# Queries of the recurrence, and keys and queries of stick-breaking attention, as seven products of quarters

## The chip, the core and the metric

One core of a Trainium2 chip runs the whole program once. The metric is device microseconds per execution. Engines: TensorE (PE; its weight loads are PEld), VectorE (DVE), ScalarE (ACT), GpSimd (POOL), and SyncE (SP), which issues the large DMA transfers. Each engine executes its own instructions in program order; engines wait for one another by semaphores.

## What is computed

Two layers of a hybrid mixer with an MLP (256 rows, width 1024, float32), then a block with three attentions and a mixture of experts. The change is in the mixer's projections of each of the two layers:

```python
h = rms_norm(x, norm_mix[l])
(sq, sk, sv, dq, dk, dv, iq, ik, iw, hq, hf, hi, hg,
 g_sb, g_dsa, g_hg) = jnp.split(h @ w_in_l, ...)
z = einsum('bqhd,bkhd->bhqk', sq, sk) * scale   # stick-breaking scores, 6 heads of 64
score = sum over 8 heads of iw * relu(iq @ ik)  # then the top 64 keys of each row
q = silu(hq); f = lb + (1 - lb) * sigmoid(hf)   # the recurrence, 4 heads of 128
```

`hq` and `hf` have 512 columns, `sk` and `sq` 384 each, and the three gates `g_*` 3072 together.

## The kernel before

The weights of `w_in` come in chunks of up to 512 columns into a ring of four slots; SyncE issues a chunk when the last reader of the chunk four before it is done (`last_use`, `used`). The order of chunks is `hf`, `hq`, `sk`, `sq`, then six gate chunks.

**Two ways to make a projection.** `feature_major` (line 1141) makes a tile of 128 features for 256 rows: eight matmuls over the depth of 1024, each 128x128 against 256 moving columns, into one PSUM bank. Each float32 matmul stands as two instructions in the trace. The other way, used for `hf` and the last eight gate tiles, is `gate_product` (line 1302): the weight is cut in four quarters (features by depth), the rows of h in four, and seven products of sums of quarters (`m1` to `m7`, in `GATE_ORDER`) replace eight. A *unit* `(c, t2)` has seven products of four matmuls with 128 moving columns, in two banks, `gy` (m1, m5, m4) and `gx` (m2, m6, m7, m3), and gives 256 features. VectorE makes the four sums of weight quarters (`gate_weight_sums`, lines 2466 to 2471) and the sums of row quarters; after a unit ScalarE copies m1 to SBUF (step `gc`), VectorE adds the products up in four instructions (`gate_corner_sums`, lines 2492 to 2498), which frees both banks, and ScalarE's step `gf` takes the corners on.

**The order.** `mixer_steps` writes one list, `MIX`, by hand, and TensorE, ScalarE and VectorE each walk it, doing what a step asks of that engine. Before the change its head is: the two units of `hf` with their corners; query tile `hq` 0; nine turns `rt` and the reversal `hj`; `hq` 1 to 3; `hp` (VectorE: forget gate); half of the first eight indexer products `ix` (128 rows against 128 keys); `sk` 0; the other half; `tk` 0 (VectorE: top 64 of the first block); `sk` 1, 2 and `sq` 0 to 2; `t5` (in layer 0 alone: a bias table, VectorE lines 2599 and 2601); eight `ix` of the second block; `tk` 1; `z`, three pairs of score products (lines 1390 and 1392); then gate columns `g` and the rest.

**What paces `ix`.** Each product goes to a bank; ScalarE puts its relu into one of two buffers (line 2016), waiting for VectorE's use of the buffer two before; VectorE multiplies by the head's weight and adds (lines 2638, 2640). The top-k is lines 2650 to 2657.

**Banks.** `Banks.give` hands out six PSUM banks in turn (`RING`); a step's first matmul waits until the user six gives before has freed its bank. Two further banks are given with `long=True`, in turn, to results that stand for longer.

**Evictions.** ScalarE takes a sigmoid of each `hq` tile (line 1982) and VectorE multiplies the tile by it (line 2595); ScalarE copies `sk` and `sq` tiles to `skT` and `sqT` (lines 1984, 1986). `z` waits for these copies.

Of the kernel before, what the change touches and what calls it, by code (L numbers as in the profile page):

```python
# [84 lines left out]
FM = {n: (n, w - 1) for n, _, w in PROJ[-4:]}  # L85
# [100 lines left out]
SEVENS = ("hf", 4, 5)  # L186
# [3 lines left out]
def mixer_steps():  # L190
# [87 lines left out]
def build(nc, a, out):  # L278
    ctx = ExitStack()
    with ctx:  # L280
# [182 lines left out]
        gate_rows_sums = [Cutter(region, REGION, at).cut(4, 4, P) for at in (at_os, at_R)]  # L463
        gate_corners = [Cutter(region, REGION, at_f + 1024 + 1024 * j).cut(8, P) for j in range(2)]

        gT_flat = gT.rearrange("p m t -> p (m t)")
        t5_onehot, t5_tab = gT_flat[0:32, 2048:3584], gT_flat[0:32, 5120:5132]
# [5 lines left out]
        def oT2(c):  # L473
# [3 lines left out]
            if c < 6:  # L477
# [58 lines left out]
         quarter_sums_ready, row_sums_ready, seven_m1_copied, seven_sigmoids) = [sem(n) for n in (  # L536
# [9 lines left out]
             "quarter_sums_ready row_sums_ready seven_m1_copied seven_sigmoids").split()]  # L546
# [35 lines left out]
        def seven_chunk(c):  # L582

            return c if c in FM else ("g", c)

        for l in range(DEPTH):
# [251 lines left out]
        def gate_weights(l, c):  # L838

            w = slot(chunk_at[(l, seven_chunk(c))])  # L840
            return [[w[:, 4 * kh:4 * kh + 4, 256 * fh:256 * fh + 256] for kh in range(2)] for fh in range(2)]

        def gate_sums(l, c):

            own_, a21 = own_quarters, gate_weights(l, c)[1][0]
            if c in ("hf", 4):
                return own_[:, 0], own_[:, 1], a21, own_[:, 2]
# [2226 lines left out]
```

## Time and profile before

| | |
|---|---|
| median of 3 runs | 1594.91 us (1593.36 to 1595.44) |
| profiled execution, span from first to last instruction | 1592.4 us (its total time is not given) |
| busy share of the span | TensorE 92%, VectorE 47%, ScalarE 20% |
| mean granted TensorE clock | 0.962 of full |

A timeline's rows merge equal instructions in a row: start, length of the stretch, engine, line, operation, output and inputs, how many, and in brackets the idle time before and what ended it. Layer 0 of the mixer lies at about 80 to 250 us, layer 1 at 550 to 720.

### The profile page before, as it was taken

The page shows a single profiled execution, that of the slowest core. Times are in us where ns is not written, and L with a number is a line of the kernel's source. Part 1 is how long each engine was busy: PE and PEld are TensorE (multiplying, and loading weights), DVE is VectorE, ACT ScalarE, POOL GpSimd, SP SyncE. Part 2 cuts the span into 40 slices and gives each one's busy share as a digit, 9 for nine tenths or more (in the row PEclk, how much of TensorE's full clock was granted, in tenths as well). Part 3 has the DMA queues.
Part 4 walks back from the last instruction along what each step waited for, and adds up shares of the span by engine and source line. Part 5 has one row for each costly group of instructions (what it writes and reads, how often), then busy time and mean ns, then how long its engine had stood idle before and what let it go on. Part 6 is the DMA issues. An engine that isn't in the chain of part 4 may idle for free.

```text
span 1592.4 us, 19689 instructions
## 1 busy us (share of the span) xinstructions
PE 1458.7 (92%) x8156; PEld 1004.4 (63%) x8156; DVE 740.9 (47%) x1465; ACT 314.6 (20%) x655; POOL 22.7 (1%) x41
## 2 busy tenths in 40 slices
PE   8999999999999999999999999999999576577578
PEld 5687889999545788898999446755554133133132
DVE  3646576766666646567666656544331000001001
ACT  2234431122001125430222001334410000000000
POOL 0000000000000000000000002100000000000000
PEclk9999999999999999999999999999999788788689
DMA  9547224454453633334444446655799999999998
GB/s 319 191 159 245 90 100 153 157 199 169 158 175 108 213 127 138 107 107 159 159 169 182 179 158 204 226 185 186 287 392 426 427 426 426 428 427 426 428 419 318
DMA packets 114921, 380.17 MB, mean 239 GB/s; under 512 B 10836, under 2 KB 23252, under 8 KB 104144
## 3 DMA queue, kind: packets, MB, share of 16 engines
q1 hardware_dynamic: 111952, 369.53, 60.6%
q0 software_dynamic: 2880, 9.36, 1.9%
q8 instruction: 67, 1.10, 0.3%
q14 instruction: 22, 0.18, 0.0%
HBM read 377.25 MB, written 5.73 MB: 241 GB/s over the span
## 4 chain that ended last, share of the span: by engine, by line
PE 79%; DMA 17%; DVE 2%; SPq 1%; ACT 1%; issue 1%; DVEq 0%; ACTq 0%
DMA ring<-in_w 17%; PE bank L1508 13%; PE bank L1561 12%; PE bank L1144 11%; PE bank L1151 8%; PE bank L1324 5%; PE bank L1712 4%; PE bank L1298 3%; PE bank L1250 3%; PE bank L1274 2%; PE bank L1610 2%; PE bank L1738 1%; PE bank L1481 1%; PE bank L1483 1%; PE bank L1200 1%; PE bank L1226 1%
## 5 line engine op out<-in xcount | busy, mean ns | idle before, releaser
L1144 PE MATMUL bank<-hT,ring 128*128 128x256 f32 x832 | 185.4, 381 | 0.0
L1144 PEld LDWEIGHTS bank<-hT,ring 128*128 128x128 f32 x832 | 156.0, 190 | 21.9 <-issue 1.0
L1712 PE MATMUL bank<-ring,region 128*32 128x512 f32 x208 | 116.4, 724 | 48.8 <-DMA region<-in_w 48.8
L1712 PE MATMUL bank<-region 128*32 128x512 f32 x512 | 116.6, 722 | 48.5 <-DMA ring<-in_w 48.5
L1561 PE MATMUL bank<-region 128*128 128x512 f32 x320 | 140.6, 592 | 0.0
L1561 PEld LDWEIGHTS bank<-region 128*128 128x128 f32 x320 | 60.5, 190 | 74.6 <-issue 74.6
L1508 PE MATMUL bank<-region 128*128 128x128 f32 x768 | 100.5, 275 | 0.0
L1508 PEld LDWEIGHTS bank<-region 128*128 128x128 f32 x768 | 93.0, 192 | 0.0
L1712 PEld LDWEIGHTS bank<-region 128*32 128x32 f32 x512 | 29.1, 130 | 94.0 <-issue 94.0
L1712 PEld LDWEIGHTS bank<-ring,region 128*32 128x32 f32 x208 | 25.8, 130 | 83.3 <-issue 83.3
L1151 PE MATMUL bank<-ring,hT 128*128 128x512 f32 x160 | 71.7, 596 | 0.0
L1771 PE MATMUL bank<-region 128*32 128x512 f32 x192 | 56.3, 684 | 15.9 <-DMA hT<-in_w 14.1
L2944 DVE TENSOR_TENSOR region<-bank,region 128x512 f32<-128x512 f32 x8 | 5.5, 692 | 139.1 <-ACT region L2113 139.1
L1508 PE MATMUL bank<-hT,ring 128*128 128x128 f32 x512 | 67.3, 275 | 0.0
L1712 PE MATMUL bank<-own_slot,region 128*32 128x512 f32 x112 | 63.4, 730 | 0.0
L1508 PEld LDWEIGHTS bank<-hT,ring 128*128 128x128 f32 x512 | 62.3, 192 | 0.1
L2954 DVE TENSOR_TENSOR region<-bank,region 128x512 f32<-128x512 f32 x8 | 5.5, 692 | 113.0 <-PE bank L1712 93.1
L1668 PEld LDWEIGHTS bank<-region,x 128*128 128x128 f32 x224 | 54.1, 335 | 5.9 <-issue 5.9
L1561 PE MATMUL bank<-ring,region 128*128 128x512 f32 x128 | 57.5, 592 | 0.0
L1151 PE MATMUL bank<-ring,region 128*128 128x456 f32 (+1 forms) x128 | 55.6, 591 | 1.4 <-ACT region L1853 1.4
L1668 PE MATMUL bank<-region,x 128*128 128x128 f32 x224 | 55.4, 405 | 0.0
L1771 PE MATMUL bank<-ring,region 128*32 128x512 f32 x256 | 54.9, 637 | 0.0
(488 smaller groups left out, 2421.6 us busy)
## 6 DMA issues: line engine op xcount, KB each, us to landing
region<-in_w SPq DMA_DIRECT2D x43, 2048.0 KB, 38.6
ring<-in_w SPq DMA_DIRECT2D x30, 2048.0 KB, 37.7
ring<-in_w_in SPq DMA_DIRECT2D x26, 2048.0 KB, 8.2
ring<-in_w_up SPq DMA_DIRECT2D x16, 2048.0 KB, 8.3
ring<-in_w_down SPq DMA_DIRECT2D x32, 1024.0 KB, 6.3
own_slot<-in_w SPq DMA_DIRECT2D x7, 2048.0 KB, 43.3
ring<-in_w_out SPq DMA_DIRECT2D x6, 2048.0 KB, 7.9
region<-in_w SPq DMA_DIRECT2D x22, 512.0 KB, 9.3
```

The lines of the kernel that those rows point to most:

```text
L1144: t = mm(b[:, 0:T], w[:, k, :], act[:, k, :], start=(k == 0), stop=(k == KD - 1))
L1151: t = mm(b[:, 0:cols], act(k)[:, i * P:(i + 1) * P], w[:, k, :], start=(k == 0), stop=(k == KD - 1))
L1250: t = mm(b, left[:, k, :], right[:, k, :], start=(k == 0), stop=(k == 3))
L1274: t = mm(b, left[:, k, :], right[:, k, :], start=(k == 0), stop=(k == 3))
L1298: t = mm(b, left[:, k, :], right[:, k, :], start=(k == 0), stop=(k == 3))
L1324: t = mm(b, left[:, k, P * t2:P * t2 + P], right[:, k, :], start=(k == 0), stop=(k == 3))
L1508: t = mm(b, left[:, k, P * t2:P * t2 + P], right[:, k, :], start=(k == 0), stop=(k == 3))
L1561: t = mm(b[:, :], left[:, t2, :], right[:, t2, :], start=(c4 == 0 and t2 == 0), stop=(c4 == 7 and t2 == 1))
L1610: t = mm(b[:, :], oT2(k)[:, i * P:(i + 1) * P], slot(chunk_at[(2, ("wo", n))])[:, k, :], start=(k == WO_FIRST), stop=(k == WO_LAST))
L1668: t = mm(b[:, P * k:P * k + P], x_rows[:, i, 4 * n + k, :], pick[:, i, :], start=(i == 0), stop=(i == NT - 1))
L1712: t = mm(b[32 * e:32 * e + 32, :], xg[:, k, 32 * e:32 * e + 32], four[e][c][:, 512 * (k % 2):512 * (k % 2) + 512], start=(k == 0), stop=(k ...
L1771: t = mm(outs[n][32 * e:32 * e + 32, :], aTq[:, c, 32 * e:32 * e + 32], w[e][:, 512 * n:512 * n + 512], start=(c == 0), stop=(c == 3))
```

## The change

The joined group `skq` treats the 384 columns of `sk` and the 384 of `sq` as the two feature halves of one weight: three units give keys and queries of two heads each. `hq` becomes two units. `hq`'s weight sums are made ahead of the list; `skq`'s in two parts (`gw`), the first between `hf`'s first and second corners, the second after the latter, since two of the sums overwrite those of `hf`. The turns and the reversal move ahead of all of `hq`. The second half of the first `ix` comes after the second `skq` unit, and the corners of the second and third `skq` units after `tk` 0. The second units of `hf` and `skq` use the two long banks. ScalarE's `gf` for `hq` is one sigmoid of 512 columns, and VectorE multiplies; for `skq` it is two copies of 256 columns out of the corners. `skq`'s corners lie in the place of the gates. The core of the diff (places of buffers, semaphores and the choice of quarters are left out):

```diff
@@ -183,7 +182,18 @@
 LAST = LEVELS - 1
-SEVENS = ("hf", 4, 5)
+SEVENS = ("hf", "hq", "skq", 4, 5)
+SEVEN_TILES = {"hf": 2, "hq": 2, "skq": 3, 4: 2, 5: 2}
+SIGMOIDS = ("hf", 4, 5)
+def seven_no(c, t2):
+    return sum(SEVEN_TILES[b] for b in SEVENS[:SEVENS.index(c)]) + t2
+SEVEN_UNITS = seven_no(SEVENS[-1], SEVEN_TILES[SEVENS[-1]])
@@ -198,14 +208,20 @@
         return [("gm", c, t2, m) for m in products]
+    def whole(c, t2):
+        return gm(c, t2, *GATE_ORDER)
+    def corners(c, t2):
+        return [("gc", c, t2), ("gf", c, t2)]
     s = []
-    s += gm("hf", 0, *GATE_ORDER) + [("gc", "hf", 0), ("gf", "hf", 0)]
-    s += gm("hf", 1, *GATE_ORDER) + [("gc", "hf", 1), ("gf", "hf", 1), ("hq", 0)]
-    s += [("rt", c) for c in range(9)] + [("hj",)] + [("hq", m) for m in range(1, 4)]
-    s.append(("hp",))
+    s += whole("hf", 0) + corners("hf", 0) + [("gw", "skq", 0)] + whole("hf", 1)
+    s += [("rt", c) for c in range(9)] + [("hj",)] + corners("hf", 1) + [("gw", "skq", 1)]
+    s += whole("hq", 0) + corners("hq", 0) + whole("hq", 1) + corners("hq", 1) + [("hp",)]
     half = N_IDX // 2
-    s += [("ix", 0, j) for j in range(half)] + [("sk", 0)] + [("ix", 0, j) for j in range(half, N_IDX)] + [("tk", 0)]
-    s += [("sk", m) for m in (1, 2)] + [("sq", m) for m in range(3)] + [("t5",)]
+    s += whole("skq", 0) + [("ix", 0, j) for j in range(half)] + corners("skq", 0)
+    s += whole("skq", 1) + [("ix", 0, j) for j in range(half, N_IDX)] + [("tk", 0)] + corners("skq", 1)
+    s += whole("skq", 2) + corners("skq", 2) + [("t5",)]
@@ -608,19 +633,18 @@
             for s in MIX:
-                if s[0] in ("rt", "hj", "ix", "hl", "hx", "ho", "oht", "o") or s[0] in FM:
+                if s[0] in ("rt", "hj", "ix", "hl", "hx", "ho", "oht", "o"):
                     bk.give((l,) + s)
-                    if s in FM.values():
-                        used((l, s[0]), (l,) + s)
...
                     if s[3] in GATE_STARTS:
-                        bk.give((l, GATE_STARTS[s[3]]) + s[1:3])
-                    if s[2:] == (1, GATE_ORDER[-1]):
-                        used((l, seven_chunk(s[1])), (l, "gy", s[1], 1))
+                        bk.give((l, GATE_STARTS[s[3]]) + s[1:3], long=s[1:3] in (("hf", 1), ("skq", 1)))
+                    if s[2:] == (SEVEN_TILES[s[1]] - 1, GATE_ORDER[-1]):
+                        for part in seven_chunks(s[1]):
+                            used((l, part), (l, "gy") + s[1:3])
@@ -1383,8 +1410,8 @@
                     elif kind == "z":
-                        c = s[1]
-                        wait_freed([(l, n, c) for n in ("sq", "sk")])
+                        c, rows = s[1], [slice(HD * hh, HD * hh + HD) for hh in range(2)]
+                        pe.wait_ge(heads_copied, 3 * l + c + 1)
@@ -1960,11 +1987,25 @@
                     elif kind == "gc":
-                        A_(gate_corners[s[2]][:, 6, :], read((l, "gy") + s[1:])[:, 0:P], ACT.Copy).then_inc(seven_m1_copied, 1)
+                        A_(seven_corners(*s[1:])[:, 6, :], read((l, "gy") + s[1:])[:, 0:P], ACT.Copy).then_inc(seven_m1_copied, 1)
+                    elif s[:2] == ("gf", "hq"):
+                        t2 = s[2]
+                        act.wait_ge(*bk.freed((l, "gy", "hq", t2)))
+                        if t2 == 0:
+                            act.wait_ge(row_corners_used, l + 1)
+                        else:
+                            act.wait_ge(hq_made, 2 * l + 1)
+                        A_(hsg_both, gate_corners[t2][:, 0:4, :].rearrange("p m t -> p (m t)"), ACT.Sigmoid).then_inc(sig_ready, 1)
+                    elif s[:2] == ("gf", "skq"):
+                        t2 = s[2]
+                        act.wait_ge(*bk.freed((l, "gy", "skq", t2)))
+                        halves = seven_corners("skq", t2)[:, 0:4, :].rearrange("p (f i) t -> p f (i t)", f=2)
+                        A_(skT[:, t2, :], halves[:, 0], ACT.Copy)
+                        A_(sqT[:, t2, :], halves[:, 1], ACT.Copy, scale=HD ** -0.5).then_inc(heads_copied, 1)
...
                         act.wait_ge(*bk.freed((l, "gy", c, t2)))
-                        dst = fT if c in FM else gT[:, 4 * c:4 * c + 4, :]
+                        dst = fT if c == "hf" else gT[:, 4 * c:4 * c + 4, :]
@@ -2457,18 +2487,27 @@
                 t.then_inc(wo_added, 1)
-            def gate_weight_sums(l, c):
-                dve.wait_ge(*arrive[chunk_at[(l, seven_chunk(c))]])
+            def gate_weight_sums(l, c, part=None):
+                for n in seven_chunks(c):
+                    dve.wait_ge(*arrive[chunk_at[(l, n)]])
...
                 s1, s2, s3, s4 = gate_sums(l, c)
-                n = 12 * l + 4 * SEVENS.index(c)
+                n = 4 * (len(SEVENS) * l + SEVENS.index(c))
+                if part == 1:
+                    dve.wait_ge(quarter_sums_ready, n + 2)
+                    V.tensor_tensor(s2, s1, a11, ALU.subtract).then_inc(quarter_sums_ready, 1)
+                    dve.wait_ge(quarter_sums_ready, n + 3)
+                    V.tensor_tensor(s4, a12, s2, ALU.subtract).then_inc(quarter_sums_ready, 1)
+                    return
...
                 dve.wait_ge(quarter_sums_ready, n + 1)
-                V.tensor_tensor(s2, s1, a11, ALU.subtract).then_inc(quarter_sums_ready, 1)
+                if part is None:
+                    V.tensor_tensor(s2, s1, a11, ALU.subtract).then_inc(quarter_sums_ready, 1)
                 V.tensor_tensor(s3, a11, a21, ALU.subtract).then_inc(quarter_sums_ready, 1)
-                dve.wait_ge(quarter_sums_ready, n + 2)
-                V.tensor_tensor(s4, a12, s2, ALU.subtract).then_inc(quarter_sums_ready, 1)
+                if part is None:
+                    dve.wait_ge(quarter_sums_ready, n + 2)
+                    V.tensor_tensor(s4, a12, s2, ALU.subtract).then_inc(quarter_sums_ready, 1)
@@ -2481,21 +2520,26 @@
             def gate_corner_sums(l, c, t2):
-                n = 6 * l + 2 * SEVENS.index(c) + t2
-                if n >= 2:
-                    dve.wait_ge(seven_sigmoids, n - 1)
+                if c == "hq":
+                    dve.wait_ge(seven_sigmoids, 6 * l + t2 + 1)
+                elif c == "skq":
+                    if t2 == 2:
+                        dve.wait_ge(heads_copied, 3 * l + 1)
+                elif (l, c) != (0, "hf"):
+                    dve.wait_ge(seven_sigmoids, 6 * l + 2 * SIGMOIDS.index(c) + t2 - 1)
+                four = seven_corners(c, t2)
                 x_, y_ = read((l, "gx", c, t2)), read((l, "gy", c, t2))
-                eight = gate_corners[t2].rearrange("p (a b) t -> p a b t", a=2)
-                pairs = gate_corners[t2].rearrange("p (a b) t -> p a b t", b=2)
+                eight = four.rearrange("p (a b) t -> p a b t", a=2)
+                pairs = four.rearrange("p (a b) t -> p a b t", b=2)
                 m5, m4 = y_[:, P:2 * P], y_[:, 2 * P:3 * P]
-                dve.wait_ge(seven_m1_copied, n + 1)
-                link(V.tensor_tensor(eight[:, :, 0, :], bc(gate_corners[t2][:, 6, :].unsqueeze(1), [2, P]),
+                dve.wait_ge(seven_m1_copied, SEVEN_UNITS * l + seven_no(c, t2) + 1)
+                link(V.tensor_tensor(eight[:, :, 0, :], bc(four[:, 6, :].unsqueeze(1), [2, P]),
                                      x_[:, 0:T].rearrange("p (a t) -> p a t", a=2), ALU.add))
-                free(V.tensor_tensor(eight[:, :, 1, :], bc(gate_corners[t2][:, 4, :].unsqueeze(1), [2, P]),
+                free(V.tensor_tensor(eight[:, :, 1, :], bc(four[:, 4, :].unsqueeze(1), [2, P]),
...
                 V.tensor_tensor(pairs[:, 0:2, 1, :], eight[:, :, 1, :], bc(m5.unsqueeze(1), [2, P]), ALU.add)
-                free(V.tensor_tensor(gate_corners[t2][:, 2, :], gate_corners[t2][:, 5, :], m4, ALU.subtract),
+                free(V.tensor_tensor(four[:, 2, :], four[:, 5, :], m4, ALU.subtract),
@@ -2578,10 +2622,11 @@
                 for i in range(NT):
-                    dve.wait_ge(sig_ready, 6 * l + i + 1)
+                    dve.wait_ge(sig_ready, 4 * l + i + 1)
...
                 t.then_inc(row_corners_used, 1)
+                gate_weight_sums(l, "hq")
@@ -2590,9 +2635,12 @@
                         free(V.tensor_copy(RT[:, s[1], :], read(key)[:, 0:T]), key)
-                    elif kind == "hq":
-                        dve.wait_ge(sig_ready, 6 * l + s[1] + 3)
-                        free(V.tensor_tensor(hqT[:, s[1], :], read(key)[:, 0:T], hsg[s[1] % 2], ALU.mult), key)
+                    elif s[:2] == ("gf", "hq"):
+                        t2 = s[2]
+                        dve.wait_ge(sig_ready, 4 * l + t2 + 3)
+                        V.tensor_tensor(hqT.rearrange("p (f t) n -> p t f n", f=2)[:, t2],
+                                        gate_corners[t2][:, 0:4, :].rearrange("p (f i) t -> p f (i t)", f=2),
+                                        hsg_both.rearrange("p (f n) -> p f n", f=2), ALU.mult).then_inc(hq_made, 1)
```

## Rows read from the trace of the kernel before

**Rows 1.** The page: busy time of the engines; granted clock in 40 slices.

```profile
PE 1458.7 (92%) x8156; PEld 1004.4 (63%) x8156; DVE 740.9 (47%) x1465; ACT 314.6 (20%) x655; POOL 22.7 (1%) x41
...
PEclk9999999999999999999999999999999788788689
```

**Rows 2.** Timeline of TensorE, layer 0: start us, us, engine, line, operation, xcount [idle before].

```profile
78.93 1.95 PE L1324 MATMUL bank<-hT,ring 128*128 128x128 f32 x16
...
91.44 3.62 PE L1144 MATMUL bank<-hT,ring 128*128 128x256 f32 x16
94.89 2.31 PE L1368 MATMUL bank<-region 128*128 128x128 f32 x18
...
97.47 10.52 PE L1144 MATMUL bank<-hT,ring 128*128 128x256 f32 x48
107.93 0.71 PE L1424 MATMUL bank<-region 64*128 64x128 f32 x8
...
131.32 2.73 PE L1381 MATMUL bank<-region 32*4 32x512 f32 x6
...
139.95 14.08 PE L1144 MATMUL bank<-hT,ring 128*128 128x256 f32 x64
```

**Rows 3.** The same for TensorE in layer 1.

```profile
550.62 1.95 PE L1324 MATMUL bank<-hT,ring 128*128 128x128 f32 x16
...
608.66 14.08 PE L1144 MATMUL bank<-hT,ring 128*128 128x256 f32 x64
```

**Rows 4.** Timeline of VectorE, layer 0.

```profile
81.63 0.17 DVE L2265 TENSOR_TENSOR small<-small 128x4 f32<-128x4 f32 x1 [7.92 <-ACT small L1953]
...
113.11 2.73 DVE L2640 SCALAR_TENSOR_TENSOR region<-region,small 128x128 f32<-128x128 f32 x7
115.87 0.23 DVE L2650 TENSOR_SCALAR region<-region 128x128 f32<-128x128 f32 x1
...
132.44 0.68 DVE L2599 TENSOR_TENSOR region<-bank,region 4x512 f32<-4x512 f32 x1 [9.41 <-PE bank L1381]
```

**Rows 5.** Timeline of VectorE, layer 1.

```profile
604.29 0.35 DVE L2638 TENSOR_SCALAR region<-region,small 128x256 f32<-128x256 f32 x1 [9.57 <-ACT region L2016]
```

**Rows 6.** Timeline of VectorE, layer 0: an add of weight quarters.

```profile
62.55 1.23 DVE L2466 TENSOR_TENSOR own_slot<-ring 128x1024 f32<-128x1024 f32 x1 [5.22 <-DMA ring<-in_w_in]
```

**Rows 7.** DMA issues within 66 to 79 and 78 to 90: count, KB, us to landing.

```profile
ring<-in_w_in SPq DMA_DIRECT2D x1, 2048.0 KB, 7.8
...
ring<-in_w_in SPq DMA_DIRECT2D x1, 1536.0 KB, 6.7
```

**Rows 8.** Timeline of all engines, layer 0: corner sums of `hf`.

```profile
85.38 0.28 ACT L1963 ACTIVATE region<-bank 128x128 f32<-128x128 f32 x1 [1.36 <-PE bank L1324]
...
85.79 0.42 DVE L2492 TENSOR_TENSOR region<-region,bank 128x256 f32<-128x256 f32 x1 [0.74 <-ACT region L1963]
...
87.04 0.28 DVE L2498 TENSOR_TENSOR region<-region,bank 128x128 f32<-128x128 f32 x1
87.36 0.63 ACT L1968 ACTIVATE region<-region 128x512 f32<-128x512 f32 x1 [0.40 <-DVE region L2498]
```

**Rows 9.** Timeline of ScalarE, layers 0 and 1.

```profile
95.43 1.14 ACT L1990 ACTIVATE region<-bank 128x256 f32<-128x256 f32 x3
...
603.80 0.66 ACT L2016 ACTIVATE region<-bank 128x256 f32<-128x256 f32 x2 [0.30 <-PE bank L1424]
```

**Rows 10.** Busy time by stretch: us, PE, PEld, DVE, ACT, POOL, PEclk, DMA, GB/s.

```profile
1224.00:1227.00 3.00, 0.91 (x10) 0.74 (x13) 1.09 (x3) 0.60 (x1) 0.00 (x0) 1.00 1.07 451
...
1243.00:1246.50 3.50, 0.00 (x1) 0.03 (x1) 0.00 (x0) 0.00 (x0) 0.00 (x0) 0.50 1.03 440
1246.50:1249.00 2.50, 2.50 (x12) 0.66 (x16) 0.00 (x0) 0.00 (x0) 0.00 (x0) 0.50 1.00 426
...
1266.00:1270.00 4.00, 3.91 (x20) 1.15 (x24) 0.00 (x0) 0.00 (x0) 0.00 (x0) 0.50 1.00 426
```

**Rows 11.** Line 1324: duration ns (min/median/max) of its weight loads.

```profile
L1324 PEld LDWEIGHTS bank<-region,ring x192: 190/192/192, 82.4 to 717.0; 128*128 128x128 f32 x192
```

More of the change, by code:

```diff
@@ L463, in build, with seven_corners @@
         gate_rows_sums = [Cutter(region, REGION, at).cut(4, 4, P) for at in (at_os, at_R)]
+        own_three = own_flat[:, 0:3072].rearrange("p (j k n) -> p j k n", j=2, k=4)
+        sbL_quarter = sbL.rearrange("p h w -> p (h w)")[:, 0:1536].rearrange("p (k n) -> p k n", k=4)
+        hsg_both = Cutter(region, REGION, at_hsg).cut(512)
         gate_corners = [Cutter(region, REGION, at_f + 1024 + 1024 * j).cut(8, P) for j in range(2)]
         gT_flat = gT.rearrange("p m t -> p (m t)")
+        head_corners = [gT_flat[:, 1024 * j:1024 * j + 1024].rearrange("p (a t) -> p a t", a=8) for j in range(2)]
+        def seven_corners(c, t2):
+            return head_corners[t2 % 2] if c == "skq" else gate_corners[t2]
         t5_onehot, t5_tab = gT_flat[0:32, 2048:3584], gT_flat[0:32, 5120:5132]
@@ L535, in build @@
          sums_ready, neg_rs_ready, up_sums_ready, h_sums_ready, m1_copied, last_half_loaded, row_quarter_sums, raw_row_sums, row_m1_copied, rows_copied, row_corners_used, wo_quarter_sums, wo_row_sums, wo_m1_copied, wo_added, p_quarter_sums, p_row_sums, p_m1_copied, p_rows_copied,
-         quarter_sums_ready, row_sums_ready, seven_m1_copied, seven_sigmoids) = [sem(n) for n in (
+         quarter_sums_ready, row_sums_ready, seven_m1_copied, seven_sigmoids, heads_copied, hq_made) = [sem(n) for n in (
              "x_late_loaded first_half_loaded down_chunk_used consts_loaded x_loaded first_loaded eps_set act_step dve_step ss_ready ffn_squared ffn_summed "
@@ L838, in gate_weights @@
         def gate_weights(l, c):
-            w = slot(chunk_at[(l, seven_chunk(c))])
+            if c == "skq":
+                return [[slot(chunk_at[(l, n)])[:, 4 * kh:4 * kh + 4, 0:384] for kh in range(2)] for n in ("sk", "sq")]
+            w = slot(chunk_at[(l, seven_chunks(c)[0])])
             return [[w[:, 4 * kh:4 * kh + 4, 256 * fh:256 * fh + 256] for kh in range(2)] for fh in range(2)]
@@ L847, in gate_sums @@
                 return own_[:, 0], own_[:, 1], a21, own_[:, 2]
+            if c == "hq":
+                return own_[:, 3], low_quarters[:, 0], a21, prT_quarter
+            if c == "skq":
+                return sbL_quarter, own_three[:, 0], a21, own_three[:, 1]
             return own_[:, 3], low_quarters[:, 0], a21, low_quarters[:, 1]
@@ L1306, in gate_product @@
                 s1, s2, s3, s4 = gate_sums(l, c)
-                r1, r2, r3, r4 = [gate_rows_sums[c not in FM][:, j] for j in range(4)]
+                r1, r2, r3, r4 = [gate_rows_sums[c in (4, 5)][:, j] for j in range(4)]
+                n = 4 * (len(SEVENS) * l + SEVENS.index(c))
                 left, right = {"m1": (a11, b11), "m2": (a12, b21), "m3": (s4, b22), "m4": (a22, r4),
@@ L1313, in gate_product @@
                             wait_freed([(l, "rsb")])
-                        arrived((l, seven_chunk(c)))
+                        for part in seven_chunks(c):
+                            arrived((l, part))
                     elif m == "m5" and c in ("hf", 4):
@@ L1317, in gate_product @@
                     if m in GATE_ORDER[2:6]:
-                        pe.wait_ge(quarter_sums_ready, 12 * l + 4 * SEVENS.index(c) + GATE_ORDER.index(m) - 1)
+                        pe.wait_ge(quarter_sums_ready, n + (3 if c == "skq" and m == "m6" else GATE_ORDER.index(m) - 1))
                 if m in GATE_STARTS:
@@ L1370, in _ @@
                         full(t, key)
-                    elif kind in FM:
-                        rows = [slice(HD * hh, HD * hh + HD) for hh in range(2)]
-                        if s[1] == 0:
-                            w = arrived((l, kind))
-                        feature_major(key, w[:, :, P * s[1]:P * s[1] + P], hT)
                     elif kind == "t5":
@@ L1975, in _ @@
                         A_(gT[:, 0:n, :], gT[:, 0:n, :], ACT.Sigmoid).then_inc(gates_ready, 1)
-                    elif kind == "hq":
-                        m = s[1]
-                        if m < 2:
-                            act.wait_ge(row_corners_used, l + 1)
-                        else:
-                            act.wait_ge(*bk.freed((l, "hq", m - 2)))
-                        A_(hsg[m % 2], read(key)[:, 0:T], ACT.Sigmoid).then_inc(sig_ready, 1)
-                    elif kind == "sk":
-                        free(A_(skT[:, s[1], :], read(key)[:, 0:T], ACT.Copy), key)
-                    elif kind == "sq":
-                        free(A_(sqT[:, s[1], :], read(key)[:, 0:T], ACT.Copy, scale=HD ** -0.5), key)
                     elif kind == "rt" and s[1] % 2 == 0:
```

12 lines of the change are left out of this document (6 added, 6 removed).

## Prediction

> **What bounds the kernel now.** I read the page first: TensorE is busy 92% of the span, VectorE 47%, and the granted clock stays near full until the last quarter [rows 1]. So up to there the order of TensorE's work is the time, and its timeline of the stretch that is changed comes next [rows 2, 3]. In layer 0 it shows the seven products of `hf` from 78.93, the turns from 94.89, three tiles of queries from 97.47, two halves of the eight `ix` products from 107.93, and the stick-breaking scores `z` ending at 139.95, where the gate columns start. TensorE waits there for about one microsecond in all. In layer 1 the same stretch runs from 550.62 to 608.66. Last comes VectorE's timeline of it: a top-k of 7.2 us from 115.87, then 9.41 us of idling until the `t5` rows arrive [rows 4], and 9.57 us at the same place in layer 1 [rows 5]. The edit spends TensorE's time less and VectorE's more, so these two idle stretches are the account it draws on.
>
> **TensorE.** A seven-product unit gives 256 features: `hf` is two of them and takes 91.44 - 78.93 = 12.51 us, so 6.25 each. A plain tile gives 128: three take 107.93 - 97.47 = 10.46, so 3.49 each [rows 2]. `hq` goes from 4 x 3.49 = 13.95 to 12.51 (-1.44), the six tiles of keys and queries from 20.92 to 3 x 6.25 = 18.76 (-2.16): -3.6 per layer, -7.2 in both. Per moving column the two forms cost the same: 112 instructions in 12.51 us are 111.7 ns at 128 columns, 48 in 10.46 are 217.9 ns at 256.
>
> The Trainium skill ("TensorE: Matmul & The Clock Gate", section "Back-to-back issue gap") says that in a stream of weight loads and matmuls both set the spacing, about 81 ns at 128 columns and 131 at 512. An estimate between these two, 98 ns at 256, would make a unit cost 1.45 times its two tiles and the edit a loss of some 31 us. The trace doesn't agree, with 111.7 against 217.9 ns for these very operands, and the rows decide.
>
> **VectorE's weight sums.** Four adds for `hq` cost 4 x 1.22 = 4.9 us [rows 6]. They stand ahead of the chain that idles until 81.63 [rows 4]; `hq` is issued with the 2 MB landing in 7.8 us [rows 7], at about 74.7, so they end near 79.5 and are hidden. If that cover were gone they would push `hf`'s first corner, which no product waits for until the fifth turn. The four adds for keys and queries have 1536 columns, not in the trace: between 1.22 (as 1024) and 2.44, taken as 1.8 by proportion. The first pair goes between the corner sums ending at 87.32 and TensorE's end of `hf`, ending near 91; it needs the query chunk, which lands in 6.7 us from 79.12, at 85.8 [rows 7]. The second pair follows `hf`'s second corner, near 100, and TensorE needs it at about 109. Both cost nothing; the price without cover is named below (late chunk).
>
> **Corner sums.** Five more per layer. One takes from 85.79 to 87.32, that is 1.53 us; ScalarE's copy of m1 goes 0.41 us ahead, and ScalarE goes on 0.04 after [rows 8]. `hq`'s two, their sigmoids and products lie under `hq` and the first key unit. `hp`, the first half of `ix` and the first key corner end about 3 us before the second half of `ix` arrives. The last two corners do not hide, because they stand behind the top-k in VectorE's order:
>
> 1. TensorE starts the second half of `ix` after six units, turns with the reversal (97.47 - 94.89 = 2.58) and the first half (0.64): 78.93 + 37.53 + 2.58 + 0.64 = 119.7 [rows 2]; layer 1: 550.62 + 40.75 = 591.4 [rows 3].
> 2. First sum of `ix` on VectorE 0.7 later, an estimate: a quarter of 0.64 for the product and 0.49 from ScalarE's start to VectorE's [rows 5, 9]; bounds 0.5 and 1.2. Four sums by 2.73 / 7 = 0.39, then the top-k of 7.2 [rows 4]: 129.2 and 600.8.
> 3. Second key corner 1.57, then ScalarE's two copies of 0.38 [rows 9], only then its copy of the next m1 (0.41), then the third corner 1.53: 4.27 us. Nearest rows are all at hand; the lower bound is 3.06 (corners back to back), the upper 4.8 (copies at the 0.63 of the 512-wide sigmoid [rows 8]).
> 4. Layer 0: `t5` starts at 133.4 instead of 132.44: +1.0. The rest of `t5`, `ix` and `z` keeps its spacing from there (132.44 to 139.95).
> 5. Layer 1 has no `t5`; ScalarE does the two last copies (0.80 with the hop) before its first `ix` relu, and VectorE follows 0.49 later: 600.8 + 4.27 + 1.29 = 606.4 instead of 604.29: +2.1.
>
> So the 3.6 us saved and the old waits turn into a TensorE wait: the second `ix` product (fifth in layer 1) needs the bank that the third key unit leaves free only with its corner sums. Sum without the clock +3.1; bounds -0.5 and +5.6. Later steps shift along: the `u` products had 1.5 us or more of cover behind VectorE, which is late by less than TensorE is.
>
> **The clock.** TensorE ends the third key unit at 126.6 and `t5` (2.7) at 129.3, does one `ix` product and waits to 133.4: 3.9 us; in layer 1 from 599.4 to 605.1: 5.7 us. After either it has only scattered small products until `z`. The mixer shows no such wait now. The nearest rows are those of the experts, in a wait for a transfer: TensorE idle, the clock is at its lower level (0.50, 1.2 GHz) through 1243 to 1246.5, and still there through 1246.5 to 1249 with TensorE busy all the time; another time through 3.9 us of work [rows 10]. A wait of 2.1 us within 1224 to 1227 left it at the upper one (1.00, 2.4 GHz). Work of 3 to 5 us (an estimate about these two rows) at half speed loses 1.5 to 2.5 us per fall; I take 2.0, twice: +4.0. Bounds 0 and 5.
>
> **DMA and queues.** No transfer is added. SyncE's waits move: the third gate chunk waits for the end of the third key unit (126.6) instead of the third key tile, some 5 us later, and is wanted over 40 us later; the second and fourth are freed earlier. POOL's stores wait for `t5` on VectorE, +1.0 us, with nothing near them. Evictions by ScalarE fall by ten and are replaced by thirteen short ones in its idle time; except in step 3 nobody waits for them.
>
> **Sum.** +3.1 + 4.0 = +7.1. The durations are of one execution whose span is 1592.4; its own total isn't given, and the span is 2.5 below the median of 1594.9, as such a span leaves out the start and end. I add the difference to the median: **1602.0 us**.
>
> **Rivals.**
> - *VectorE is in time* (faster). If the third key corner ends before 132.4 and 603.0, TensorE runs through: seven units of 6.25 (43.8), the turns (2.6), two halves of `ix` (1.3), and from `t5` to the gates the 8.6 of now less 0.6 of waiting need 55.7 where 61.0 pass [rows 2]: -5.3, and about -5 in layer 1: 1584.6. The point is VectorE's idle of 9.41 and 9.57 [rows 4, 5]. Against it: step 1 delays the top-k by 6.2 and step 3 adds 4.3, together 10.5. Chance 0.13.
> - *The clock stays up.* Same chain, no fall: 1598.0, with the bounds 1594.4 to 1600.5. For it: the row with a wait of 2.1 us at 1.00; against it: the rows of the long wait, and that here only scattered products follow. Chance 0.20.
> - *Late chunk.* The sums of the joined group stand in VectorE's queue ahead of its copies of turns; each microsecond that the query chunk lands after 86 delays turns and all of the chain one for one. One or two more: 1603 to 1604. Rows put the landing at 85.8. Chance 0.05.
> - *Narrow products don't pay*, so the change doesn't do what it says: were each instruction paced by its weight load, 0.192 us [rows 11], a unit would take 10.75, and both layers lose 38 us: 1633. Rows of `hf` speak against it. Under 0.01. The rule of the Trainium skill above would come near this case.
>
> **Numbers.** Main case 0.58, the rivals above, 0.03 for nothing at all moving. The range is 1595 to 1605: it takes in the main case and most of the unthrottled one, and leaves out the faster rival and the tails, about 0.2. A measurement of this kernel tells 0.2% (3.2 us) from no change. Faster 0.13; same 0.20 (half of the second rival, the low edge of the main case, no effect); slower 0.67. Within the slower cases alone 1599 to 1605.
>
> **What would show it.** Right: seven-product units of 6.25 us for `hq` and the joined group; TensorE idle 4 and 6 us ahead of `ix` of the second block, released by VectorE's corner sums (line 2498 before) or ScalarE's relu; VectorE with no idle of 9 us there; gate columns starting 62 to 65 and 60 to 63 us after `hf`'s first product (61.0 and 58.0 now); the granted clock at 0.5 around there. Wrong: VectorE idle left before the last corner sums, gates starting before 138 and 606, or TensorE's units slower than 6.3 us.

## The result, and the profile after

The changed kernel takes **1598.17 us** (median of 10 runs, 1596.30 to 1599.82); the kernel before took 1594.17 beside it. The ratio is 1.0026, 95% interval 1.0018 to 1.0034: slower by a quarter of a per cent. The time lies within the predicted range; the forecast of 1602.0 was 3.8 us too high. The profiled execution's span is 1596.5 (before 1592.4), so the trace holds the whole difference of 4.1 us.

The page, against [rows 1]: TensorE is busy 1.5 us longer, VectorE 37.6 us longer, and the fourth slice of the granted clock, 120 to 160 us, is an 8.

```profile
PE 1460.2 (91%) x8396; PEld 1009.9 (63%) x8396; DVE 778.5 (49%) x1517; ACT 316.1 (20%) x661; POOL 22.7 (1%) x41
...
PEclk9998999999999999999999999999999788788789
```

TensorE's timeline in layer 0, against [rows 2]:

```profile
79.03 1.95 PE L1356 MATMUL bank<-hT,ring 128*128 128x128 f32 x16
...
106.44 1.95 PE L1356 MATMUL bank<-hT,ring 128*128 128x128 f32 x16
...
119.88 0.72 PE L1451 MATMUL bank<-region 64*128 64x128 f32 x8
...
126.97 2.73 PE L1408 MATMUL bank<-region 32*4 32x512 f32 x6
129.64 0.81 PE L1451 MATMUL bank<-region 64*128 64x256 f32 x2
133.96 4.76 PE L1451 MATMUL bank<-region 64*128 64x256 f32 x14 [3.52 <-DVE region L2542]
...
141.49 14.08 PE L1174 MATMUL bank<-hT,ring 128*128 128x256 f32 x64
```

The `t5` products start at 126.97 where they started at 131.32: TensorE has gained its time, 4.35 us with an old wait. Then it waits 3.52 us for VectorE, and the gate columns, 61.02 us behind the first product of `hf` before (139.95 - 78.93), are now 62.46 behind it. Layer 1 shows the same, against [rows 3]:

```profile
552.15 1.95 PE L1356 MATMUL bank<-hT,ring 128*128 128x128 f32 x16
...
606.80 2.51 PE L1451 MATMUL bank<-region 64*128 64x256 f32 x8 [5.57 <-DVE region L2542]
...
612.43 14.08 PE L1174 MATMUL bank<-hT,ring 128*128 128x256 f32 x64
```

The distance is 60.28 instead of 58.04. So the two layers lose 1.44 and 2.24 us up to the gate columns; with 0.1 ahead of layer 0's `hf` and 0.3 behind layer 1's gate columns that is the span's 4.1. (These two small differences say nothing: in the profiled executions below, `hf` starts anywhere from 77.97 to 79.34, and from layer 1's gate columns to the end 983.1 to 985.3 us pass.) VectorE shows why (layer 0, against [rows 4]); L2688 are the sums of `ix`, L2698 begins a top-k, L2536 a key unit's corner sums, L2647 the rows of `t5`:

```profile
87.34 1.75 DVE L2503 TENSOR_TENSOR region<-ring 128x1536 f32<-128x1536 f32 x1
...
120.77 1.51 DVE L2688 SCALAR_TENSOR_TENSOR region<-region,small 128x128 f32<-128x128 f32 x4 [3.94 <-ACT region L2046]
122.32 0.23 DVE L2698 TENSOR_SCALAR region<-region 128x128 f32<-128x128 f32 x1
...
129.80 0.42 DVE L2536 TENSOR_TENSOR region<-region,bank 128x256 f32<-128x256 f32 x1 [0.31 <-DVE region L2705]
...
132.37 0.42 DVE L2536 TENSOR_TENSOR region<-region,bank 128x256 f32<-128x256 f32 x1 [1.05 <-ACT region L1990]
...
133.82 0.67 DVE L2647 TENSOR_TENSOR region<-bank,region 4x512 f32<-4x512 f32 x1
...
136.96 0.33 DVE L2686 TENSOR_SCALAR region<-region,small 128x256 f32<-128x256 f32 x1
```

In the kernel before, the second-block sums of layer 0 started here:

```profile
135.59 0.34 DVE L2638 TENSOR_SCALAR region<-region,small 128x256 f32<-128x256 f32 x1
```

The idle 9.41 us are gone. The top-k starts at 122.32 instead of 115.87, both corner sums stand behind it, and the `t5` rows come at 133.82 instead of 132.44. Between the corner sums VectorE is idle for 1.05 us: ScalarE copies the next m1 only after the two copies of keys and queries. In layer 1 (against [rows 5]) the same hop stands once more ahead of the sums:

```profile
605.22 0.42 DVE L2536 TENSOR_TENSOR region<-region,bank 128x256 f32<-128x256 f32 x1 [1.05 <-ACT region L1990]
...
607.81 0.35 DVE L2686 TENSOR_SCALAR region<-region,small 128x256 f32<-128x256 f32 x1 [1.06 <-ACT region L2046]
```

The granted clock in layer 0 by microsecond (us, PE, PEld, DVE, ACT, POOL, PEclk, DMA, GB/s), which [rows 10] stood in for:

```profile
129.00:130.00 1.00, 1.00 (x4) 0.29 (x2) 0.66 (x3) 0.00 (x0) 0.00 (x0) 1.00 0.96 360
130.00:131.00 1.00, 0.44 (x2) 0.00 (x0) 0.93 (x3) 0.00 (x0) 0.00 (x0) 0.55 1.04 408
...
139.00:140.00 1.00, 1.00 (x10) 0.94 (x8) 0.93 (x3) 0.72 (x3) 0.00 (x0) 0.50 0.51 176
140.00:141.00 1.00, 1.00 (x13) 0.93 (x12) 0.93 (x3) 1.00 (x3) 0.00 (x0) 0.83 0.04 14
141.00:142.00 1.00, 1.00 (x10) 0.84 (x7) 0.93 (x3) 0.98 (x2) 0.64 (x1) 1.00 0.08 16
```

It falls to 0.50 (1.2 GHz) and is back at 1.00 as the gate columns start. The forecast put the fall down to the wait. In layer 0 that is not so: TensorE was busy until 130.44, and a mean of 0.55 over 130 to 131 puts the fall near 130.1, ahead of the wait. In layer 1, where TensorE is idle from 601.2, the clock stood at 1.00 until 604 and fell within the wait:

```profile
604.00:605.00 1.00, 0.00 (x0) 0.00 (x0) 0.17 (x1) 0.80 (x3) 0.00 (x0) 0.78 1.05 410
```

### The profile page after: what moved, and what is told of

Its sections match the earlier page's. It is cut to its first block, busy times and chain, and to the rows that moved or that the text cites. A ratio compares the mean times of both kernels' runs of the same rounds, so it can differ in the third digit from the quotient of the medians.

```text
span 1596.5 us, 20231 instructions
## 1 busy us (share of the span) xinstructions
PE 1460.2 (91%) x8396; PEld 1009.9 (63%) x8396; DVE 778.5 (49%) x1517; ACT 316.1 (20%) x661; POOL 22.7 (1%) x41
## 4 chain that ended last, share of the span: by engine, by line
PE 78%; DMA 17%; DVE 2%; SPq 1%; ACT 1%; issue 0%; DVEq 0%; ACTq 0%
DMA ring<-in_w 17%; PE bank L1535 13%; PE bank L1588 12%; PE bank L1356 8%; PE bank L1181 8%; PE bank L1174 7%; PE bank L1739 4%; PE bank L1328 3%; PE bank L1280 3%; PE bank L1304 2%; PE bank L1637 2%; PE bank L1765 1%; PE bank L1508 1%; PE bank L1510 1%; PE bank L1230 1%; PE bank L1256 1%
## 5 line engine op out<-in xcount | busy, mean ns | idle before, releaser
L1739 PE MATMUL bank<-ring,region 128*32 128x512 f32 x208 | 115.3, 718 | 50.2 <-DMA region<-in_w 50.2
L1739 PE MATMUL bank<-region 128*32 128x512 f32 x512 | 115.5, 718 | 42.9 <-DMA ring<-in_w 42.9
L1174 PE MATMUL bank<-hT,ring 128*128 128x256 f32 x512 | 114.6, 381 | 0.0
L1174 PEld LDWEIGHTS bank<-hT,ring 128*128 128x128 f32 x512 | 95.7, 190 | 13.5 <-issue 1.0
L1798 PE MATMUL bank<-region 128*32 128x512 f32 x192 | 61.7, 745 | 16.0 <-DMA hT<-in_w 14.2
L1535 PEld LDWEIGHTS bank<-hT,ring 128*128 128x128 f32 x512 | 62.3, 192 | 0.1
L1798 PE MATMUL bank<-ring,region 128*32 128x512 f32 x256 | 60.2, 683 | 0.0
```

The costliest lines, as they stand in the source:

```text
L1174: t = mm(b[:, 0:T], w[:, k, :], act[:, k, :], start=(k == 0), stop=(k == KD - 1))
L1535: t = mm(b, left[:, k, P * t2:P * t2 + P], right[:, k, :], start=(k == 0), stop=(k == 3))
L1739: t = mm(b[32 * e:32 * e + 32, :], xg[:, k, 32 * e:32 * e + 32], four[e][c][:, 512 * (k % 2):512 * (k % 2) + 512], start=(k == 0), stop=(k ...
L1798: t = mm(outs[n][32 * e:32 * e + 32, :], aTq[:, c, 32 * e:32 * e + 32], w[e][:, 512 * n:512 * n + 512], start=(c == 0), stop=(c == 3))
```

## Experiments

My theory was: VectorE's row (first-block `ix` sums, top-k, two corner sums with a hop to ScalarE) sets the second-block `ix` sums, and the lower clock costs little, because the products under it are paced by relu and sums. The rivals were the clock itself at 2 us a layer, and that one of the two groups doesn't pay. The nine further kernels were timed in five rounds each, e_best a second time as e_best2. The last two columns are the start of the gate columns behind the first product of `hf`, against the kernel before, in the profiled execution.

| kernel | median us | ratio to before | layer 0 | layer 1 |
|---|---|---|---|---|
| changed kernel | 1598.17 | 1.0026 [1.0018, 1.0034] | +1.44 | +2.24 |
| e_fill | 1597.43 | 1.0018 [1.0009, 1.0027] | +1.27 | +1.99 |
| e_hop | 1597.82 | 1.0018 [1.0009, 1.0027] | +0.93 | +1.98 |
| e_hop_fill | 1595.80 | 1.0009 [0.9999, 1.0018] | +0.12 | +0.84 |
| e_hq_only | 1598.01 | 1.0024 [1.0014, 1.0034] | +0.92 | +2.61 |
| e_hq_long | 1600.34 | 1.0042 [1.0029, 1.0056] | +0.93 | +2.58 |
| e_skq_only | 1600.68 | 1.0044 [1.0030, 1.0058] | +3.40 | +3.48 |
| e_early | 1594.56 | 0.9999 [0.9990, 1.0008] | -0.65 | -0.53 |
| e_before_early | 1593.00 | 0.9997 [0.9988, 1.0006] | -1.17 | -0.99 |
| e_best | 1587.11 | 0.9960 [0.9946, 0.9974] | -1.96 | -3.47 |
| e_best2 | 1587.23 | 0.9960 [0.9946, 0.9974] | -3.58 | -3.46 |

**The clock's price in the changed kernel.** Extra products fill TensorE's wait:

```diff
 t = mm(b[:, 0:wide], RT[r, 4 + j // 2, i * P:(i + 1) * P], RT[r, 8, 0:wide], start=True, stop=True)
+if i == 1 and j == (0, 3)[l]:
+    for k in range((8, 12)[l]):
+        t = mm(b[:, T:2 * T], hT[:, k % KD, 0:P], hT[:, (k + 1) % KD, :], start=True, stop=True)
 full(t, key)
```

> The changed kernel with 8 (layer 0) and 12 (layer 1) extra products of the rows with themselves, which nothing reads, put into TensorE's wait ahead of the second-block index products (about 3.5 and 5.2 us of work in waits of 3.5 and 5.6 us); they go to the unused half of a bank, and that bank's relu waits for them. Theory A, from the trace of the changed kernel: the half clock behind the wait falls on products that are paced by ScalarE and VectorE anyway, so a clock kept at 1.00 gives back only 0.2 us in each layer: 0.4 us less, not to be told from no change in the runs, and the gate columns 0.1 to 0.3 us earlier after the index sums in the trace. Theory B, the clock term of the prediction: 2.0 us in each layer, 4.0 us less (ratio 0.9975) against the changed kernel.

In layer 1 the clock now stays at 1.00, and the gate columns start 0.25 us earlier behind `hf` (612.12 - 552.09 = 60.03); in layer 0 it still falls, with the fillers running, and 0.17 comes back:

```profile
130.00:131.00 1.00, 1.00 (x3) 0.35 (x3) 0.93 (x3) 0.00 (x0) 0.00 (x0) 0.50 1.05 410
```

Together 0.42: theory A. The runs agree, with intervals that overlap the changed kernel's. TensorE's timeline in layer 1 shows why it is so little; the changed kernel's first `z` products (L1417), then e_fill:

```profile
609.25 1.23 PE L1417 MATMUL bank<-region 64*128 64x256 f32 x4
```

```profile
606.74 0.70 PE L1451 MATMUL bank<-region 64*128 64x256 f32 x4 [0.20 <-DVE region L2545]
607.77 0.97 PE L1451 MATMUL bank<-region 64*128 64x256 f32 x4 [0.32 <-ACT region L2049]
609.18 0.70 PE L1417 MATMUL bank<-region 64*128 64x256 f32 x4 [0.45 <-ACT region L2049]
...
612.12 14.08 PE L1174 MATMUL bank<-hT,ring 128*128 128x256 f32 x64
```

At half speed `z` starts 57.10 us behind `hf` (609.25 - 552.15), at full speed 57.09 (609.18 - 552.09): what TensorE then gains on the `ix` products it waits for the relu (L2049). In layer 0 both start 59.35 behind it (138.38 and 138.48). Only the `z` products themselves come faster.

**The hop.** The list puts both m1 copies ahead of the key copies, and the third unit's products ahead of the top-k:

```diff
-    s += whole("skq", 1) + [("ix", 0, j) for j in range(half, N_IDX)] + [("tk", 0)] + corners("skq", 1)
-    s += whole("skq", 2) + corners("skq", 2) + [("t5",)]
+    s += whole("skq", 1) + [("ix", 0, j) for j in range(half, N_IDX)] + whole("skq", 2) + [("tk", 0)]
+    s += [("gc", "skq", 1), ("gc", "skq", 2), ("gf", "skq", 1), ("gf", "skq", 2), ("t5",)]
```

> The changed kernel, but ScalarE makes both last m1 copies before either pair of key and query copies, and top-k 0 stands behind the third unit's products in the written order; every engine does the same work. Theory A, the second-block index sums are bound by VectorE's row of top-k 0 and two corner sums: its idle 1.05 us between the two corner sums vanishes in each layer, the t5 rows start near 132.8 instead of 133.8 and layer 1's index sums near 606.8 instead of 607.8: 2.1 us less (ratio 0.9987). Theory B, TensorE and its clock set the time: at most 0.3 us less.

The second-block sums do come 1.14 and 1.15 us earlier behind `hf` (135.95 - 79.16 and 606.29 - 551.78), as theory A has it. The gate columns gain only 0.51 and 0.26, and the run's time can't be told from the changed kernel's. TensorE's timeline, layer 1, shows what is late next:

```profile
607.73 1.23 PE L1417 MATMUL bank<-region 64*128 64x256 f32 x4
...
609.14 1.09 PE L1417 MATMUL bank<-region 64*128 64x256 f32 x4
...
610.42 1.09 PE L1417 MATMUL bank<-region 64*128 64x256 f32 x4
...
611.80 14.08 PE L1174 MATMUL bank<-hT,ring 128*128 128x256 f32 x64
```

The `z` products come without a wait, 1.41 and 1.28 us apart: TensorE, at half clock, has become their pace. The next run puts the loop of e_fill into e_hop, with as many products as the shorter waits hold:

```diff
+    for k in range((4, 9)[l]):
```

> The kernel with the m1 copies moved ahead (e_hop), with 4 (layer 0) and 9 (layer 1) extra products that nothing reads put into TensorE's wait. In e_hop the index products came 1.1 us earlier and the gate columns only 0.3 to 0.5 us. Theory A, the half clock took the rest: the z products stand 1.28 us apart at half clock and 1.04 at full, so with the clock kept up layer 1's gate columns start 46.5 us after the turns instead of 47.5 and layer 0's at 48.6 to 49.2 instead of 49.4: about 1.3 us less than e_hop, 2.3 less than the changed kernel. Theory B, the pace of relu and sums took it: no difference from e_hop.

```profile
607.10 0.70 PE L1417 MATMUL bank<-region 64*128 64x256 f32 x4 [0.45 <-ACT region L2049]
...
608.14 0.70 PE L1417 MATMUL bank<-region 64*128 64x256 f32 x4
...
609.18 0.70 PE L1417 MATMUL bank<-region 64*128 64x256 f32 x4
...
610.03 14.08 PE L1174 MATMUL bank<-hT,ring 128*128 128x256 f32 x64
```

1.04 apart again, and both layers gain 1.95 us together against e_hop (0.81 and 1.14); the runs fall by 2.02. Theory A, and more than it asked. So, by one profiled execution of each kernel, the lower clock costs 0.42 us where VectorE is the later one and 1.95 where VectorE is 1.1 us earlier: the two are rivals for the same microseconds, not terms of one sum.

**One group alone.** First the recurrence queries (the keys and queries as whole tiles, as in the kernel before):

```diff
-SEVENS = ("hf", "hq", "skq", 4, 5)
+SEVENS = ("hf", "hq", 4, 5)
...
-    s += whole("skq", 0) + [("ix", 0, j) for j in range(half)] + corners("skq", 0)
...
+    s += [("ix", 0, j) for j in range(half)] + [("sk", 0)] + [("ix", 0, j) for j in range(half, N_IDX)] + [("tk", 0)]
+    s += [("sk", m) for m in (1, 2)] + [("sq", m) for m in range(3)] + [("t5",)]
```

> The changed kernel with the recurrence queries as quarter products, but the stick-breaking keys and queries as whole tiles in the order of the kernel before. Theory A, the VectorE chain of the joined keys and queries is what costs: without their corner sums the idle time of VectorE ahead of the second-block index sums covers the little that the recurrence queries add, and TensorE's 1.44 us a layer come through: 2.9 us less than the kernel before, 6.9 less than the changed one (1591.3; ratio to the kernel before 0.9982). Theory B, quarter products at 128 columns bring nothing or the weight sums delay something for either group: same as the kernel before or slower.

Theory A fell: the runs are slower than the kernel before, which is theory B's outcome, though for neither of its reasons. TensorE's timeline shows two waits, and layer 1's five tiles behind them at a lower clock (0.50 from 588 to 591; the tiles took 17.53 us before):

```profile
108.73 3.69 PE L1175 MATMUL bank<-hT,ring 128*128 128x256 f32 x16 [1.47 <-DVE region L2551]
...
114.48 0.48 PE L1456 MATMUL bank<-region 64*128 64x128 f32 x2 [1.42 <-ACT region L2055]
...
587.50 19.22 PE L1175 MATMUL bank<-hT,ring 128*128 128x256 f32 x80
```

The first names the corner sums, as if a bank were missing. The next run gives one (`long=s[1:3] in (("hf", 1), ("hq", 1))`):

> The kernel with the recurrence queries alone as quarter products (e_hq_only), but their second tile in the two spare banks. Theory A, in e_hq_only TensorE's 1.44 us a layer were eaten by its wait of 1.47 us for the bank of the second tile (its corner sums end 2 us behind its last column) and by the relu wait and the clock behind it: with the spare banks both waits go and 2.9 us come through, 1591.3 (ratio to the kernel before 0.998). Theory B, the quarter products of the recurrence queries bring nothing in themselves: no difference from the kernel before, or slower.

This fell too: no gain either, in the trace or in the runs. (The profiled execution, 1597.54, is the fastest of five; the other four took 1599.7 to 1601.8, and no trace shows why.) The first wait is gone and the second has taken all of it:

```profile
114.34 0.48 PE L1456 MATMUL bank<-region 64*128 64x128 f32 x2 [2.93 <-ACT region L2055]
```

It waits for a relu, and the relu for the sums, which in e_hq_only start at 113.83 behind the second tile's corner sums (107.05), the product with the sigmoid and the recurrence gate's steps. The account of layer 0 is 1.47 + 1.42 - 0.51 (the old wait) - 1.44 = +0.94, measured +0.92, and with spare banks 2.93 - 0.51 - 1.44 = +0.98, measured +0.93. So the bank is not the cause; by the trace it is VectorE's row behind the second tile, busy from 109.28 to the sums but for 0.16 us, which no run of this kernel changed. In the changed kernel two key units, 12.5 us, stand between the second query unit and the second half of `ix`, where e_hq_only has one tile of 3.49, and VectorE waits 3.94 us there (120.77 above).

Then the other group alone, the recurrence queries' tiles where they were:

```diff
-SEVENS = ("hf", "hq", "skq", 4, 5)
+SEVENS = ("hf", "skq", 4, 5)
...
-    s += whole("hq", 0) + corners("hq", 0) + whole("hq", 1) + corners("hq", 1) + [("hp",)]
+    s += [("hq", m) for m in range(1, 4)] + [("hp",)]
```

> The changed kernel with the joined keys and queries as quarter products and the recurrence queries as four whole tiles, as before. Theory A, VectorE's row from the first-block index products to the third key corner sums sets the second-block index sums, and only TensorE's work ahead of that row can move it: the recurrence queries' 1.44 us come back ahead of it in each layer and TensorE's 2.16 us of the keys fall into its wait: the gate columns start 1.4 us later after the first gate product than in the changed kernel, 2.9 us more than the changed kernel (1601; ratio to the kernel before 1.0043). Theory B, the two groups add as TensorE's work does: 2.16 us a layer less than the kernel before, 1590 (0.9973).

Theory A: 1600.68 and 1.0044, and 3.20 us more than the changed kernel up to the gate columns (1.96 and 1.24). The saving on the recurrence queries, ahead of VectorE's row, comes through; the larger one on keys and queries, behind it, falls into the wait.

**Giving VectorE the time.** It is idle while the recurrence queries are computed; the first-block products need only the turns:

```diff
-    s += whole("hq", 0) + corners("hq", 0) + whole("hq", 1) + corners("hq", 1) + [("hp",)]
+    s += whole("hq", 0) + [("ix", 0, j) for j in range(half)] + corners("hq", 0)
+    s += whole("hq", 1) + [("ix", 0, j) for j in range(half, N_IDX)] + corners("hq", 1) + [("tk", 0), ("hp",)]
...
-    ... long=s[1:3] in (("hf", 1), ("skq", 1)))
+    ... long=s[1:3] in (("hf", 1), ("hq", 1), ("skq", 1)))
```

> The changed kernel with the first-block index products moved ahead, four behind each tile of the recurrence queries, and top-k 0 behind the second tile, where VectorE waits; the second tile of the recurrence queries goes to the spare banks. Same work on every engine. Theory A, top-k 0 on VectorE in the last 7.2 us before the key corner sums is what held the second-block index sums: they start near 131.8 in layer 0 instead of 137.0 and near 603 in layer 1 instead of 607.8: 9 to 10 us less than the changed kernel (1588 to 1589), 5 to 6 less than the kernel before, and TensorE's waits of 3.5 and 5.6 us go. Theory B, the clock carries 4 us of it: 13 to 14 us less. Theory C, top-k 0 is not the cause (corner sums and copies alone hold it): 2 us less or no change.

Half of what theory A asked: 4.9 us up to the gate columns, 3.6 in the runs. My row for VectorE had forgotten the gate's steps (`hp`, 3.9 us) behind the top-k, and two of the hops; TensorE still waits 2.43 us in layer 1 and its clock falls. The next kernel takes these out:

```diff
+    s += whole("hq", 0) + [("ix", 0, j) for j in range(half)] + corners("hq", 0) + [("hp",)]
+    s += whole("hq", 1) + [("ix", 0, j) for j in range(half, N_IDX)] + [("gc", "hq", 1), ("tk", 0), ("gf", "hq", 1)]
+    s += whole("skq", 0) + [("gc", "skq", 0)] + whole("skq", 1) + [("gc", "skq", 1), ("gf", "skq", 0), ("gf", "skq", 1), ("t5",)]
+    s += whole("skq", 2) + [("gc", "skq", 2)] + [("ix", 1, j) for j in range(2)] + [("gf", "skq", 2)]
+    s += [("ix", 1, j) for j in range(2, N_IDX)] + [("tk", 1)]
```

> The changed kernel with four moves, same work on every engine: first-block index products behind the tiles of the recurrence queries, top-k 0 right behind them, the recurrence gate's VectorE steps ahead of them in VectorE's idle time, both early key units' m1 copies ahead of the first copies of keys, the bias products and rows ahead of the third key unit, and two relus ahead of the last copies of keys. Theory A, VectorE's row ahead of the second-block index sums is the bound: the sums start about 37 us after the turns in layer 1 (changed kernel 43.2) and about 40 in layer 0 (45.4), TensorE waits under 1 us there and its clock stays at 1.00, so the gate columns start 5 us earlier in each layer: 10 us less than the changed kernel (1588), 6 less than the kernel before (ratio 0.996). Theory B, a row of ScalarE or VectorE behind the sums takes it back: the gate columns start earlier, but the u products wait for VectorE, and 4 us or less are left against the changed kernel.

> The kernel with the four moves (e_best) once more, for a second set of runs: 1587 to 1588, ratio to the kernel before 0.995 to 0.997.

1587.11 and, in the second set, 1587.23: theory A, and faster than both kernels. Up to the gate columns layer 1 gains 5.7 us on the changed kernel in both profiled executions, layer 0 3.4 and 5.0: the clock did not stay up there in the first (last section). VectorE in layer 1 of e_best, then TensorE:

```profile
597.39 0.42 DVE L2536 TENSOR_TENSOR region<-region,bank 128x256 f32<-128x256 f32 x1 [4.31 <-ACT region L1990]
...
598.84 0.34 DVE L2686 TENSOR_SCALAR region<-region,small 128x256 f32<-128x256 f32 x1
```

```profile
598.97 1.13 PE L1451 MATMUL bank<-region 64*128 64x256 f32 x8 [0.96 <-DVE region L2542]
...
603.51 14.08 PE L1174 MATMUL bank<-hT,ring 128*128 128x256 f32 x64
```

VectorE has its idle time back ahead of the last corner sums, where it waits for TensorE's unit by way of ScalarE's copy, and TensorE waits 0.96 instead of 5.57. The last run asks whether the order alone does this, by giving the whole-tile kernel the same order:

```diff
-    s += [("hq", m) for m in range(1, 4)] + [("hp",)]
...
+    s += [("hq", 1)] + [("ix", 0, j) for j in range(half)] + [("hq", 2)] + [("ix", 0, j) for j in range(half, N_IDX)]
+    s += [("hq", 3), ("tk", 0), ("hp",)]
+    s += [("sk", m) for m in range(3)] + [("sq", m) for m in range(2)] + [("t5",), ("sq", 2)]
```

> The kernel before (whole tiles) with the same moves as far as it has the steps: first-block index products among the recurrence queries, top-k 0 and the recurrence gate behind them, the bias products ahead of the last query tile. Theory A, VectorE was idle for 9.4 us there, so top-k 0 is moved within cover and only the bias rows leave the path: 1.0 to 1.4 us less in layer 0, nothing in layer 1: 1593. The larger part of what e_best gains over the kernel before is then the quarter products' own. Theory B, the order alone makes e_best's gain: 5 to 6 us less here too.

1593.00, the ratio not told from 1: theory A's time, but not for its reason. In layer 1 the trace gains 0.99, which I had at nothing: the second half of `ix` takes 0.64 us instead of 1.63, without its relu wait. Layer 0 has the same gain (0.64 instead of 1.64), so of its 1.17 us only about 0.2 are left for the bias rows, which I had at 1.0 to 1.4. So in the same order, as far as the whole-tile kernel has the steps, the quarter products are worth 5.9 us of the 7.2 that TensorE saves.

## Why the prediction was right, and which term was not

- **TensorE: right.** Each unit takes 6.25 us (93.94 to 106.44 for two), and -3.6 a layer is there. The Trainium skill ("TensorE: Matmul & The Clock Gate", section "Back-to-back issue gap") would have made narrow products dearer per column; the trace of the new units does not show that at 128 columns: 12.50 us for 112 instructions are 111.6 ns each, against 217.9 at 256.
- **Weight sums: right.** 1.75 us each (taken as 1.8), without a wait for the query chunk ahead of them; the late chunk did not happen. From layer 0's gate columns to layer 1's `hf` pass 410.66 us (before 410.67).
- **Steps 1 to 5: right.** Second half of `ix` at 119.88 (119.7), top-k ended near 129.5 (129.2), `t5` rows at 133.82 (133.4). The second-block sums are 1.27 and 1.99 us later behind `hf`: 3.26 against the sum of 3.1. That they stand behind the top-k is shown by e_early and e_best, which move it, and by e_skq_only.
- **The waits: right**, 3.52 and 5.57 us for 3.9 and 5.7, released by the corner sums as said. **What brings the clock down: wrong in layer 0.** It fell there before the wait began, and in e_fill without any wait; only layer 1's fall belongs to a wait, and e_fill's products took it away.
- **The clock's price: the term that failed.** "Work of 3 to 5 us (an estimate about these two rows) at half speed loses 1.5 to 2.5 us per fall; I take 2.0, twice: +4.0." It measured 0.42 (e_fill). The rows of the experts show TensorE at work at the lower clock, not that the work would have ended earlier at full speed. Here that work was `ix` and `z`: `ix` is held back by relu and sums, so that `z` starts at the same place at either clock, and the clock was up again when the gate columns began. The term took half speed for lost time without asking what else paces the work. So the forecast of +7.1 was +4.0 beside the kernel before, and 1598.17 lies just below the 1599 to 1605 given for the slower cases. That the rival *the clock stays up*, 1598.0, is met to 0.2 us is luck: the clock did fall, its sum was +3.1, and the median that it was added to, 1594.9, is 0.7 above the 1594.17 measured beside the changed kernel. e_hop_fill shows when the term counts, 1.95 us, once VectorE's row is 1.1 us earlier.
- *VectorE in time* gave 1584.6; made true by order alone it is 1587.1.

Left open: which of the four moves of e_best brings how much. They were not tried one by one, but for the first (e_early, with the gate's steps still behind it). What brings layer 0's clock down is open too (last section).

## What to carry to other kernels

A saving on the busiest engine counts only up to the next place where it meets another engine's row: list that row with everything queued in it, hops included, and move work from behind the meeting point into the idle time ahead of it before shortening products. Costs that fall into the same wait, here VectorE's lateness and a lower clock, are compared, not added: the later one counts and the other appears when the first is removed. A wait names the last releaser only; giving it what it names (a bank) can move the whole wait one step on.

## Not expected of the hardware

In layer 0 of the changed kernel the clock is at 1.2 GHz from about 130.1 until past 140, in e_fill from 129.9 to 133.3: seven microseconds more at half speed cost 0.17 us. And the clock can fall with TensorE busy all through: in e_fill it stood at 0.50 from 130 to 133 while fillers ran (the row above). The fall came within 1 us of the end of the `t5` products, 2.73 us of 32 rows by 4 columns, in the changed kernel, e_fill, e_hop_fill and e_best. But behind the same products it stayed at 1.00 in the kernel before and in e_best2, so that they are the cause is a guess that no run tests. Two executions of one kernel differ here. Timeline and clock of e_best, then of e_best2, at the first two products of the unit behind `t5`:

```profile
120.90 2.73 PE L1408 MATMUL bank<-region 32*4 32x512 f32 x6
123.56 3.67 PE L1356 MATMUL bank<-hT,ring 128*128 128x128 f32 x16
```

```profile
125.00:126.00 1.00, 1.00 (x7) 1.00 (x7) 0.99 (x2) 0.00 (x0) 0.00 (x0) 0.50 0.00 0
```

```profile
119.75 2.73 PE L1408 MATMUL bank<-region 32*4 32x512 f32 x6
122.41 2.05 PE L1356 MATMUL bank<-hT,ring 128*128 128x128 f32 x16
```

```profile
123.00:124.00 1.00, 1.00 (x12) 1.00 (x11) 0.96 (x3) 0.00 (x0) 0.00 (x0) 1.00 0.00 0
```

3.67 us at a granted clock of 0.50 and 2.05 at 1.00: this is layer 0's difference of 1.6 us between the two in the table. A wait doesn't settle it either: in e_hq_long TensorE waits the same 2.93 us in both layers, and behind it the clock stays at 1.00 in layer 0 (114 to 120) and is at 0.50 in layer 1 (588 to 590). So a fall seen in one profiled execution can be missing in the next, and its price with it.
